# A two-layer decoder trunk: three sub-layer boundaries taken one token tile at a time, the feed-forward in blocks of 512, attention in pairs of heads

## The chip, the cores and the metric

The kernel runs on one core of a Trainium2 chip. TensorE (PE) multiplies, VectorE (DVE) and ScalarE (ACT) do the elementwise work and empty PSUM, GpSimd (POOL) does little, and SyncE (SP) issues nearly all weight loads. PSUM has eight banks, ps0 to ps7, of 128 x 512 floats. The metric is the device time in microseconds (us), the median of several runs; the time before is 1700.63 us.

## The reference, cut to what matters

The input is one sequence of 256 tokens of 1024 floats, so there are two tiles (t = 0, 1) of 128 tokens. All is float32.

```python
# layer 0
u = modulate(rms_norm(x, g_mix[0]), shift, scale)        # shift, scale, gate from c @ w_ada + b_ada
y = concat([dilated_attention(q, k, v), s5_mixer(s_in)]) @ w_out     # 8 heads of 64
x = x + gate * y
u = modulate(rms_norm(x, g_ffn[0]), shift, scale)
x = x + gate * ((silu(u @ w_gate) * (u @ w_up)) @ w_down)            # 1024 -> 2816 -> 1024
# layer 1
u = modulate(rms_norm(x, g_mix[1]), shift, scale)
x = x + gate * (sparse_attention(u @ w_in) @ w_out)      # indexer picks 64 keys, 16 heads of 64
u = modulate(rms_norm(x, g_ffn[1]), shift, scale)
x = x + gate * mixture_of_experts(u)                     # router picks 2 of 8 experts
out = rms_norm(x, g_final)
```

## The kernel before, in words

It is written engine by engine: each engine has its own program in a fixed order, and semaphores tie them together. The order of the work on an engine is the order of its code.

- **Weights.** SP loads items of up to 2 MB into a ring of five slots. A slot is loaded again once its last user has signalled. For the plain float32 projections the signal is `weights_used`, sent by the first PE instruction after the last use (`release`).
- **Split products.** The dense feed-forward, the input projection of layer 1 and the experts multiply in a rounded 32-bit format with three products (`mm3`, L783 to L785). Each weight chunk (a quarter of an item) is split by ACT into `w_hi` (`high`, L1492) and by DVE into `w_lo` (`low`, L1803). There are four chunk buffers, so chunk q can be split only when PE has finished chunk q-4 (`chunk_done`). The other products are plain float32.
- **Modulation vectors.** `c @ w_ada` comes in 24 pieces. `matvec` (L808, L814) multiplies one piece with four groups of 32 columns of the PE array, `part_out` on ACT copies the sums out, and `columns_of` (L822) or `gate_of` (L828) on PE spreads them. The pieces are sown between other work: one beside each head of layer 0, one beside every second head of layer 1, four around the end of the dense feed-forward.
- **A head of attention.** `scores` (PE, L867, contraction over 64 rows), `mask_max` (DVE), `exps` (ACT, L1505), `weights_sum` (DVE), `probs` (ACT, L1514), `probsT` (PE transposes, L789), `probsT_out` (ACT, L1526), `weigh` (PE, L891 to L893, into 64 of the 128 output partitions). Even heads use the lower 64 rows or partitions, odd heads the upper 64. The softmax buffer `sm` has three places, scores go to ps0 and ps1 in turn, and two heads fill one bank that `head_out` copies.
- **A sub-layer boundary.** The last projection ends in four groups of matmuls, one for each token tile and half of the columns. `residual` (DVE, L1885, L1887) multiplies by the gate into an SBUF buffer and adds to `h`. `norm_stats` (ACT) waits for all four, squares and sums both tiles (L1457) and takes both roots (L1460). `norm_scale` (DVE, L1814) scales both tiles, `norm` (PE) transposes 16 blocks of 128, `norm_split` (DVE, L1828) applies the modulation in eight instructions of 256 columns, `norm_hi` (ACT, L1485) and DVE (L1832) split the result into `x_hi` and `x_lo`, and then the split products begin. In front of the router `norm_out` shares the modulation between ACT and DVE, and nothing is split.
- **The dense feed-forward.** 2816 columns in eight blocks of 352. For each block: gate product, up product, silu and product, transposes, down product (three row groups of 128, 128 and 96).
- **The end.** After the experts both tiles are added up, both are normalised, and one store of 1 MB writes the output.

## Time and profile before

| what | us |
|---|---|
| median of three runs | 1700.63 (1700.23 to 1701.93) |
| the profiled execution | 1697.09 |
| its span | 1695.3 |
| PE busy | 1583.3 (93%) |
| DVE busy | 1265.8 (75%) |
| ACT busy | 1045.0 (62%) |

The chain that ended last runs over PE for 81% of the span. About 1000 us of it, from 668 us on, are the experts, where the PE row shows 24.3 to 25 us busy in each 25 us. The first 668 us hold layer 0, the dense feed-forward and the attention of layer 1, with gaps at the boundaries. "PEclk" is the clock granted to TensorE, as a share of its full speed. A plain float32 matmul appears as two records in the trace.

### The profile page before, as it was taken

What the parts mean: (1) busy time and instruction counts of PE and PEld (TensorE: products, weight loads), DVE (VectorE), ACT (ScalarE), POOL (GpSimd) and SP (SyncE); (2) the same over time, 40 slices, a digit from 0 to 9 for tenths busy, and PEclk for the clock granted to TensorE, in tenths of its full rate; (3) what the DMA queues carried; (4) which work ended last, traced back from release to release, by engine and by line L of the source; (5) the groups of instructions that cost most, each with busy time, mean ns of one, the idle gap of its engine ahead of it and who ended that gap; (6) DMA issues with size and microseconds to landing.
All of it is one profiled execution on the core that took longest, in us unless ns stands there. A gap on an engine that the chain in (4) does not pass through costs nothing.

```text
span 1695.3 us, 22996 instructions
## 1 busy us (share of the span) xinstructions
PE 1583.3 (93%) x7839; PEld 1248.8 (74%) x7840; DVE 1265.8 (75%) x1764; ACT 1045.0 (62%) x1401; POOL 62.5 (4%) x90
## 2 busy tenths in 40 slices
PE   4999979999897986999999999999999999999996
PEld 2645479998784535888888888888888888888884
DVE  6895154554545215989989989989989989989986
ACT  3105154443333624778778778778778778778774
POOL 5341000000000000000000000000000000000000
PEclk9999989999888996999999999999999999999998
DMA  9626555554662745999999989999999999989960
GB/s 322 218 98 246 212 194 171 190 185 167 201 224 100 257 147 196 330 338 367 356 332 366 357 328 365 352 331 372 345 335 374 344 335 368 360 325 363 356 229 26
DMA packets 208055, 469.66 MB, mean 277 GB/s; under 512 B 5316, under 2 KB 26102, under 8 KB 207878
## 3 DMA queue, kind: packets, MB, share of 16 engines
q1 hardware_dynamic: 206960, 466.80, 76.2%
q0 software_dynamic: 400, 1.09, 0.3%
q10 hardware_dynamic: 646, 1.16, 0.2%
q8 instruction: 27, 0.44, 0.1%
q14 instruction: 22, 0.18, 0.0%
HBM read 467.98 MB, written 1.05 MB: 277 GB/s over the span
## 4 chain that ended last, share of the span: by engine, by line
PE 81%; DVE 5%; ACT 4%; issue 2%; DVEq 0%; ACTq 0%
PE ps L783 22%; PE ps L785 21%; PE ps L784 21%; PE ps L789 3%; PE ps L1287 2%; PE ps L808 2%; DVE w_lo L1803 2%; PE ps L853 2%; PE ps L1058 2%; ACT work L1699 1%; PE ps L867 1%; PE ps L822 1%; ACT w_hi L1492 1%; PE ps L1356 1%; PE ps L1357 1%
## 5 line engine op out<-in xcount | busy, mean ns | idle before, releaser
L1803 DVE TENSOR_TENSOR w_lo<-ring,w_hi 128x1024 fp32r<-128x1024 f32 (+4 forms) x600 | 672.8, 1155 | 92.0 <-ACT w_hi L1492 79.4
L1492 ACT ACTIVATE w_hi<-ring 128x1024 fp32r<-128x1024 f32 (+4 forms) x600 | 601.3, 1008 | 216.7 <-PE ps L785 214.4
L783 PE MATMUL ps<-w_hi,e_hi 128*128 128x512 f32 x896 | 356.3, 398 | 9.7 <-DVE w_lo L1803 9.7
L785 PE MATMUL ps<-w_hi,e_lo 128*128 128x512 f32 x896 | 350.4, 391 | 0.0
L784 PE MATMUL ps<-w_lo,e_hi 128*128 128x512 f32 x896 | 349.6, 390 | 0.0
L1803 DVE TENSOR_TENSOR w_lo<-ring_more,w_hi 128x1024 fp32r<-128x1024 f32 x192 | 229.0, 1222 | 40.5 <-ACT w_hi L1492 38.1
L1492 ACT ACTIVATE w_hi<-ring_more 128x1024 fp32r<-128x1024 f32 x192 | 201.6, 1067 | 70.8 <-PE ps L785 70.8
L783 PEld LDWEIGHTS ps<-w_hi,e_hi 128*128 128x128 f32 x896 | 168.7, 188 | 46.3 <-DVE w_lo L1803 13.2
L785 PEld LDWEIGHTS ps<-w_hi,e_lo 128*128 128x128 f32 x896 | 168.6, 188 | 36.6
L784 PEld LDWEIGHTS ps<-w_lo,e_hi 128*128 128x128 f32 x896 | 168.8, 188 | 33.5
L783 PE MATMUL ps<-w_hi,eT_hi 128*128 128x512 f32 x448 | 176.7, 394 | 5.6 <-DVE w_lo L1803 5.6
L785 PE MATMUL ps<-w_hi,eT_lo 128*128 128x512 f32 x448 | 174.7, 390 | 0.0
L784 PE MATMUL ps<-w_lo,eT_hi 128*128 128x512 f32 x448 | 174.5, 390 | 0.0
L783 PE MATMUL ps<-w_hi,x_hi 128*128 128x352 f32 (+5 forms) x352 | 116.7, 332 | 9.5 <-DVE x_lo L1832 4.6
L785 PE MATMUL ps<-w_hi,x_lo 128*128 128x352 f32 (+5 forms) x352 | 115.4, 328 | 0.0
L784 PE MATMUL ps<-w_lo,x_hi 128*128 128x352 f32 (+5 forms) x352 | 115.3, 328 | 0.0
L783 PEld LDWEIGHTS ps<-w_hi,eT_hi 128*128 128x128 f32 x448 | 84.1, 188 | 28.3 <-DVE w_lo L1803 11.8
L785 PEld LDWEIGHTS ps<-w_hi,eT_lo 128*128 128x128 f32 x448 | 84.1, 188 | 18.1
L784 PEld LDWEIGHTS ps<-w_lo,eT_hi 128*128 128x128 f32 x448 | 84.2, 188 | 16.6
L783 PEld LDWEIGHTS ps<-w_hi,x_hi 128*128 128x128 f32 x352 | 69.0, 196 | 11.5 <-DVE x_lo L1832 4.9
L784 PEld LDWEIGHTS ps<-w_lo,x_hi 128*128 128x128 f32 x352 | 69.0, 196 | 0.9
L785 PEld LDWEIGHTS ps<-w_hi,x_lo 128*128 128x128 f32 x352 | 68.8, 196 | 0.7
(286 smaller groups left out, 1674.1 us busy)
## 6 DMA issues: line engine op xcount, KB each, us to landing
ring<-in_moe_w_gate SPq DMA_DIRECT2D x48, 2048.0 KB, 10.0
ring<-in_moe_w_up SPq DMA_DIRECT2D x40, 2048.0 KB, 10.2
ring<-in_moe_w_down SPq DMA_DIRECT2D x32, 2048.0 KB, 10.0
ring<-in_w_ada SPq DMA_DIRECT2D x24, 2048.0 KB, 8.4
ring_more<-in_moe_w_down SPq DMA_DIRECT2D x24, 2048.0 KB, 7.9
ring_more<-in_moe_w_up SPq DMA_DIRECT2D x16, 2048.0 KB, 10.0
ring_more<-in_moe_w_gate SPq DMA_DIRECT2D x8, 2048.0 KB, 9.3
ring<-in_ff_w_gate SPq DMA_DIRECT2D x8, 1408.0 KB, 6.5
```

The costliest lines, as they stand in the source:

```text
L783: mm(o, xh, wh, start=start, stop=False)
L784: mm(o, xh, wl, start=False, stop=False)
L785: return mm(o, xl, wh, start=False, stop=stop)
L789: return nc.tensor.transpose(o, i, ident[0:n, 0:n])
L808: w = mm(ps[bank][j:j + 32, :], c_col[:, k:k + 1].broadcast_to([P, 32]), ap[:, k, :], start=k < 4, stop=False, tile_position=(0, j))
L822: w = mm(ps[bank][:, c + q:c + q + 1], part[:, q * P:(q + 1) * P], sel_col, start=True, stop=True)
L853: w = mm(ps[banks[t]][:, 0:n], xT[:, k, t * P:(t + 1) * P], ap[:, k, 0:n], start=k == 0, stop=k == KD - 1)
L867: w = mm(ps[n % 2][:, KOFF[t]:KOFF[t] + KEYS[t]], qT_[r, hh // 2, t * P:(t + 1) * P], kT_[r, hh // 2, 0:KEYS[t]], start=True, stop=True)
L1058: w = mm(ps[2 * n + t][:, :], catT[:, k, t * P:(t + 1) * P], ap[:, k, :], start=k == 4, stop=k == 3)
L1287: w = mm(o, hn[:, t, d], sel[:, t, :], start=t == 0, stop=t == NT - 1)
L1492: fn(w, src, ACT.Copy).then_inc(hi_ready, 1)
L1803: V.tensor_tensor(w_lo[0:n, c, 0:f], src, w_hi[0:n, c, 0:f].bitcast(F32), ALU.subtract).then_inc(lo_ready, 1)
```

## The change

1. **Heads in pairs.** `scores_pair` issues the scores of an even and an odd head in turn, into ps0 and ps1; `weigh_pair` does the same for the weighted sums. DVE and ACT do `weights_sum`, `mask_max`, `exps`, `probs` of two heads one after the other.
2. **Boundaries by tile.** Residual, squares, root, scaling, transposes, modulation and split are done for tile 0 and then for tile 1. The output projections finish both halves of tile 0 first, and the transposes of tile 0 stand before the last group. The gate product of the first feed-forward block, the first projection of layer 1 (`rows_of`) and the router run by tile. ACT squares and takes roots tile by tile, with a root of a constant ahead (`roots`). The gate product of the residual stays in PSUM.
3. **The feed-forward** is cut into five blocks of 512 columns and one of 256.
4. **Four modulation pieces** change places: two go to the start of the feed-forward, the other two to its end.
5. **The end** is done by tile, with two stores of 512 KB.

```diff
-FB = 8
-FW = FF // FB
-FT = [(0, P), (P, P), (2 * P, FW - 2 * P)]
+FW = 512
+FB = (FF + FW - 1) // FW
+FL = FF - (FB - 1) * FW
...
+            def scores_pair(n, qT_, kT_, pair, first=False):
+                if not first:
+                    pe.wait_ge(max_ready, n)
                 for t in range(NT):
...
+                    for i in range(2):
+                        r = slice(HD * i, HD * i + HD)
+                        w = mm(ps[i][:, KOFF[t]:KOFF[t] + KEYS[t]], qT_[r, pair, t * P:(t + 1) * P],
+                               kT_[r, pair, 0:KEYS[t]], start=True, stop=True)
...
+            def weigh_pair(n, v, pair, cat0):
+                pe.wait_ge(pT_ready, n + 2)
...
+                for cols, keys, tile_, first, last_ in (...):
+                    for i in range(2):
+                        hd = slice((2 * pair + i) * HD, (2 * pair + i + 1) * HD)
+                        w = mm(o[HD * i:HD * i + HD, cols], v[:, tile_, hd], pT[:, (n + i) % 2, keys], start=first, stop=last_)
+                w.then_inc(o_done, 2)
...
-            e_out_part(0, (0, 1, 2, 3))
-            pending[0] = True
-            e_out_part(1, (0, 1, 2, 3))
-            pending[0] = True
-            norm(1)
+            pe.wait_ge(gate_ready, 4)
+            e_out_part(0, 0, (0, 1, 2, 3))
+            e_out_part(1, 0, (0, 1, 2, 3))
+            e_out_part(0, 1, (0, 1, 2, 3))
+            norm(1, 0, 4)
+            e_out_part(1, 1, (0, 1, 2, 3))
+            pending[0] = 2
+            matvec(12, 2)
...
-            rows(ff_first["gate"][2], (0, 1), FW, range(NCI), 0)
+            rows_of(ff_first["gate"][2], 0, FW, 0, 1)
+            norm(1, 1, 4)
+            rows_of(ff_first["gate"][2], 1, FW, 1, 1)
+            matvec(13, 6)
+            pe.wait_ge(part_ready, 13)
             rows(ff_first["up"][2], (2, 3), FW, range(NCI))
+            pe.wait_ge(part_ready, 14)
...
             pe.wait_ge(silu_done, FB * NT)
-            matvec(12, 0)
-            matvec(13, 1)
-            ff_T((FB - 1) * NT)
-            ff_down(ff_last["down"][2], (FB - 1) * NT, False, True)
-            pe.wait_ge(part_ready, 14)
             matvec(14, 0)
             matvec(15, 1)
-            pe.wait_ge(h_ready, 8)
+            ff_T((FB - 1) * NT, FL)
+            ff_down_last(ff_last["down"][2], (FB - 1) * NT)
+            pe.wait_ge(part_ready, 16)
...
+            o_out_part(0, 0)
+            o_out_part(1, 0)
+            o_out_part(0, 1)
+            norm(3, 0)
+            o_out_part(1, 1)
+            pending[0] = 2
+            norm(3, 1)
+            pe.wait_ge(late_in, 16 * 2)
+            router(0)
+            router(1).then_inc(router_done, 1)
...
+            def roots():
+                fn(stat[:, 30:31], eps[:, 0:1], ACT.Sqrt)
...
             item_high(ff_first["gate"][2], *ff_first["gate"][:2], ff_chunk_of(FW))
-            norm_hi(1)
+            roots()
+            for t in range(NT):
+                act.wait_ge(h_ready, 2 * t + 2)
+                rms(h[:, t, :], hn[:, t, :], D, t)
+                if t:
+                    part_out(12, parts1[:, 0, :], 2)
+                norm_hi(1, t)
+            part_out(13, parts1[:, 1, :], 6)
             item_high(ff_first["up"][2], *ff_first["up"][:2], ff_chunk_of(FW))
...
-            residual(4, 0, 0, None, 0)
-            norm_scale(1, 2)
-            dve.wait_ge(mod_ready, 2)
             item_low(ff_first["gate"][2], ff_first["gate"][0], ff_chunk_of(FW))
-            norm_split(1)
+            for t in range(NT):
+                residual(t, 4, 0, (t, 2 + t), 0)
+                dve.wait_ge(h_ready, 2 * t + 2)
+                norm_scale(1, t, 3 + t)
+                dve.wait_ge(mod_ready, 2)
+                norm_split(1, t)
...
-            sp.dma_start(out_tok, final_y).then_inc(out_stored, 16)
+            for t in range(NT):
+                sp.wait_ge(y_final, t + 1)
+                sp.dma_start(out_tok[:, t, :], final_y[:, t, :]).then_inc(out_stored, 16)
```

The first place is the middle of the head loop of layer 1 on PE, two heads before the change. (ada is the buffer of the turned queries, keys and values, uT holds the softmax, work the modulation sums.)

```order
L867 MATMUL ps0<-ada_50 128x128
L867 MATMUL ps0<-ada_50 128x256
L891 MATMUL ps5<-uT_49,ada_50 64x128
L892 MATMUL ps5<-uT_49,ada_50 64x128
L893 MATMUL ps5<-uT_49,ada_50 64x128
L789 MATMUL ps2<-cst,uT_49 128x128 x3
L867 MATMUL ps1<-ada_50 128x128
L867 MATMUL ps1<-ada_50 128x256
L891 MATMUL ps4<-uT_49,ada_50 64x128
L892 MATMUL ps4<-uT_49,ada_50 64x128
L893 MATMUL ps4<-uT_49,ada_50 64x128
L822 MATMUL ps7<-cst,work_52 128x1 x4
```

And the same place after the change, one pair of heads:

```order
L808 MATMUL ps6<-ring,c_col 32x512 x8
L814 MATMUL ps6<-bias_rows,cst 32x128 x4
L858 MATMUL ps0<-ada_50 128x128
L858 MATMUL ps1<-ada_50 128x128
L858 MATMUL ps0<-ada_50 128x256
L858 MATMUL ps1<-ada_50 128x256
L884 MATMUL ps4<-uT_49,ada_50 64x128 x6
L789 MATMUL ps2<-cst,uT_49 128x128 x3
L822 MATMUL ps7<-cst,work_52 128x1 x4
L789 MATMUL ps3<-cst,uT_49 128x128 x3
```

The scores of both heads (L858) now stand side by side, in ps0 and ps1 by turns, and so do the six products with the values (L884).

The second place is PE from the end of the output projection of layer 0 to the first feed-forward products, before the change:

```order
L1058 MATMUL ps0<-ring,ada_50 128x512 x4
L1058 MATMUL ps1<-ring,ada_50 128x512 x4
L1058 MATMUL ps2<-ring,ada_50 128x512 x4
L1058 MATMUL ps3<-ring,ada_50 128x512 x4
L789 MATMUL ps0<-cst,work_52 128x128 x2
```

After it (L1056 is the same projection; L808 and L814 are the modulation piece 12):

```order
L1056 MATMUL ps0<-ring,ada_50 128x512 x4
L1056 MATMUL ps2<-ring,ada_50 128x512 x4
L1056 MATMUL ps1<-ring,ada_50 128x512 x4
L789 MATMUL ps4<-cst,work_52 128x128 x4
L789 MATMUL ps5<-cst,work_52 128x128 x4
L1056 MATMUL ps3<-ring,ada_50 128x512 x4
L808 MATMUL ps2<-ring,c_col 32x512 x8
L814 MATMUL ps2<-bias_rows,cst 32x128 x4
```

Tile 0 (ps0 and ps2) is finished first, its transposes go in before the last group (ps3), and a modulation piece follows.

The third place is ACT at the same boundary, after the change (L1504 is the root of a constant, L1499 squares, L1501 takes roots, L1532 modulates, L1541 splits the activations, L1490 copies modulation sums):

```order
L1504 ACT_TABLE_LOAD
L1504 ACTIVATE stat<-eps 128x1
L1499 ACTIVATE work_52,stat<-h 128x1024
L1501 ACTIVATE stat<-stat,eps 128x1
L1532 ACTIVATE uT_49<-ps4,mod_b,mod_a 128x128 x4
L1541 ACTIVATE x_hi_56<-uT_49 128x4x128 x2
L1499 ACTIVATE work_52,stat<-h 128x1024
L1501 ACTIVATE stat<-stat,eps 128x1
L1490 ACTIVATE ada_50<-ps2 128x512
L1532 ACTIVATE uT_49<-ps6,mod_b,mod_a 128x128 x4
L1541 ACTIVATE x_hi_56<-uT_49 128x4x128 x2
L1490 ACTIVATE ada_50<-ps6 128x512
```

The function table is loaded before the squares and not between squares and root, and the copy of piece 13 (L1490 from ps6) is the last of these rows; the split of the first up item comes behind it (L1548, four instructions).

## Rows read from the trace of the kernel before

**Rows 1.** Windows: start:end, length, busy PE PEld DVE ACT POOL, clock, DMA, GB/s.
```profile
211.79:226.24 14.45, 3.59 (x17) 3.28 (x17) 10.52 (x20) 9.81 (x18) 0.00 (x0) 0.72 0.53 190
226.24:413.38 187.14, 187.14 (x1062) 176.60 (x1062) 93.87 (x136) 82.61 (x133) 0.00 (x0) 0.99 0.56 186
421.34:431.37 10.03, 10.03 (x36) 7.80 (x36) 2.19 (x3) 0.58 (x2) 0.00 (x0) 0.83 0.70 227
431.37:449.86 18.49, 12.09 (x98) 8.96 (x97) 13.79 (x28) 10.37 (x20) 0.00 (x0) 0.82 0.87 294
541.95:604.08 62.13, 59.17 (x408) 34.16 (x408) 13.93 (x93) 40.95 (x132) 0.00 (x0) 0.91 0.67 233
631.86:648.62 16.76, 9.01 (x48) 8.68 (x48) 4.86 (x9) 6.98 (x11) 0.62 (x1) 0.68 0.44 157
1675.50:1690.10 14.60, 3.63 (x9) 2.48 (x8) 8.21 (x12) 5.03 (x8) 0.00 (x0) 0.73 0.01 3
```

**Rows 2.** Timeline of PE, heads of layer 0: start, us, instruction, idle before.
```profile
133.31 0.93 PE L867 MATMUL ps<-ada 64*128 64x128 f32 x8 [0.83 <-ACT ada L1551]
...
150.34 1.92 PE L808 MATMUL ps<-ring,c_col 128*32 128x512 f32 x16
...
152.42 0.92 PE L867 MATMUL ps<-ada 64*128 64x128 f32 x4
153.27 0.43 PE L891 MATMUL ps<-uT,ada 128*64 128x128 f32 x2
...
154.07 1.05 PE L822 MATMUL ps<-cst,work 128*128 128x1 f32 x8
154.98 0.53 PE L789 MATMUL ps<-cst,uT 128*128 128x128 f32 x3
155.44 1.92 PE L808 MATMUL ps<-ring,c_col 128*32 128x512 f32 x16
```

**Rows 3.** Timeline of PE, the modulation pieces of layer 1's second and last pair.
```profile
551.06 2.63 PE L808 MATMUL ps<-ring,c_col 128*32 128x512 f32 x16
...
595.62 1.92 PE L808 MATMUL ps<-ring,c_col 128*32 128x512 f32 x16
```

**Rows 4.** Timeline of ACT, one head of layer 1, from probsT_out to probs.
```profile
570.97 0.50 ACT L1526 ACTIVATE uT<-ps 128x384 f32<-128x384 f32 x1
...
572.22 0.80 ACT L1514 ACTIVATE uT<-uT,stat 128x128 f32<-128x128 f32 x2
```

**Rows 5.** Timeline of all engines at the boundary to the feed-forward.
```profile
213.24 1.06 ACT L1457 ACTIVATE work<-h 128x1024 f32<-128x1024 f32 x1 [21.45 <-DVE h L1887]
...
215.44 1.28 ACT L1460 ACT_TABLE_LOAD   x1
216.74 0.30 ACT L1460 ACTIVATE stat<-stat,eps 128x2 f32<-128x2 f32 x1
...
221.81 3.70 DVE L1828 TENSOR_SCALAR uT<-ps,mod_a,mod_b 128x256 f32<-128x256 f32 x8
...
225.43 2.76 DVE L1832 TENSOR_TENSOR x_lo<-uT,x_hi 128x256 fp32r<-128x256 f32 x8
```

**Rows 6.** Timeline of PE, split products of 512 and of 256 columns.
```profile
421.65 0.39 PE L784 MATMUL ps<-w_lo,mT_hi 128*128 128x512 f32 x1
421.88 0.40 PE L785 MATMUL ps<-w_hi,mT_lo 128*128 128x512 f32 x1
...
453.70 0.28 PE L784 MATMUL ps<-w_lo,x_hi 128*128 128x256 f32 x1
453.82 0.28 PE L785 MATMUL ps<-w_hi,x_lo 128*128 128x256 f32 x1
```

**Rows 7.** DMA issues by line: count, KB each, median us from issue to landing.
```profile
ring<-in_w_ada SPq DMA_DIRECT2D x24, 2048.0 KB, 8.4
...
out<-work SPq DMA_DIRECT2D x1, 1024.0 KB, 4.8
```

**Rows 8.** The page's costliest groups: the split of weights on DVE and ACT.
```profile
L1803 DVE TENSOR_TENSOR w_lo<-ring,w_hi 128x1024 fp32r<-128x1024 f32 (+4 forms) x600 | 672.8, 1155 | 92.0 <-ACT w_hi L1492 79.4
L1492 ACT ACTIVATE w_hi<-ring 128x1024 fp32r<-128x1024 f32 (+4 forms) x600 | 601.3, 1008 | 216.7 <-PE ps L785 214.4
```

More of the change, by code:

```diff
@@ L1487, in high, with norm_hi @@
+            def norm_hi(n, t):
+                norm_out(n, t, 4)
+                act.wait_ge(uT_ready, KD * (2 * n + t))
+                for half in range(2):
+                    ks, ts = slice(4 * half, 4 * half + 4), slice(t * P, (t + 1) * P)
+                    fn(x_hi[:, ks, ts], uT[:, ks, ts], ACT.Copy).then_inc(x_hi_ready, 1)
             def high(q, c, src, n=P):
@@ L1557, in _ @@
             th = lambda c: hn.rearrange("p t d -> p (t d)")[:, c * S:(c + 1) * S]
[L1558 to L1566 removed]
+            exps(1, False)
+            for pair in range(A_HEADS // 2):
+                a = 2 * pair
+                probs(a)
+                probs(a + 1)
+                if pair:
+                    part_out(4 + a - 1, parts_b[:, 1, :], 6, a - 1 if a >= 3 else 0)
+                if pair == 3:
+                    gate_out(0, 0, 7, 6)
+                if pair == 0:
                     for c in range(4):
@@ L2065, in _ @@
+            for t in range(NT):
+                dve.wait_ge(h_ready, 4 + 2 * t + 2)
+                norm_scale(2, t, 5 + t)
+            columns(0, 1, 10, 2)
             dve.wait_ge(mod_ready, 3)
```

615 lines of the change are left out of this document (315 added, 300 removed).

## The prediction, made before the change was run

> **What bounds the kernel now.** I read the windows by stage first. PE is busy in all of the 187.14 us of the feed-forward, and in 59.17 of the 62.13 us from the first head product of layer 1 to its output projection; in the four stretches between sub-layers it is busy 3.6 of 14.45, 12.1 of 18.49, 9.0 of 16.76 and 3.6 of 14.60 us [rows 1]. So a gain comes either from PE's own instructions becoming fewer or shorter, or from the chains over DVE and ACT that stand in those four gaps. The timeline of PE then shows what a head is made of [rows 2, 3], that of ACT how long the softmax chain is [rows 4], and that of all engines what stands in a gap [rows 5]. The experts, some 1000 us, are not touched: PE-bound before and after, so nothing is booked there.
>
> The profiled execution took 1697.1 us, 3.5 less than the median of 1700.6. The sum is made against the first and carried to the second.
>
> **Heads of layer 0.** One head takes 5.10 us of PE (150.34 to 155.44): the modulation piece 2.08, scores 0.85, weighted sum 0.80, columns 0.91, transposes 0.46 [rows 2]. Do two heads' scores really run beside each other? The trace has it once: where heads 0 and 1 stand next to each other, eight records take 0.93 us, and four records of a single head take 0.92 [rows 2]. The upper and the lower 64 rows overlap fully. The modulation piece gives the same for output columns: its 16 records of 512 columns go to four groups of 32 columns and take 1.92 us in all [rows 2], while one plain float32 product of 512 columns, moved as four passes at the 0.2275 us of a split product [rows 6], would be 0.9 us, and eight of them 7. So a pair saves one scores and one weighted sum, 0.85 + 0.80. Three pairs of scores in the loop and four weighted sums: 5.8 us. Against it, in the middle pairs DVE has two reciprocal blocks in one piece and ACT copies modulation sums only after both heads' probabilities, so the second piece of a pair starts late; I take 0.7 us twice. Bounds: no overlap and these waits (+1.4), or full overlap and none (-5.8). Value -4.3, near the row that shows the overlap.
>
> **Heads of layer 1.** Six pairs take 44.56 us (551.06 to 595.62), 7.43 each [rows 3]. PE's content falls by 1.65 to 5.7. But now the chain counts: probsT_out to probs of one head is 2.05 us on ACT [rows 4], and ACT does, from the last transpose of a pair, probsT_out 0.4, exps twice 1.8, head_out 0.3, probs twice 1.4, part_out 0.5, in all 4.4, before PE may do the columns (0.9) and the last transposes (0.5): 5.9 with the handovers. The pair period is 5.9: 6 x 1.5 = 9.2 us. At the start the first weighted sum moves into the next pair and the clock is low (0.91 over the stretch [rows 1]): 2.5 us; at the end 0.4. Value -12.1; bounds -14.0 (5.7 per pair) and -1 (no overlap).
>
> **Feed-forward.** A split product of 512 columns follows its forerunner after 0.23 us (0.2275 over long runs), one of 256 after 0.12 [rows 6]. After: gate and up 480 x 0.2275 + 96 x 0.12 = 120.7, five down products 240 x 0.2275 = 54.6, forty transposes at 0.1, together 179.3. Before: 187.14 at a mean clock of 0.99, which is 1.9 lost to the low clock [rows 1], so 185.2. Value -5.9. DVE is 94 of 187 us busy and the DMA share 0.56 [rows 1], which hides the larger items; bounds -4 and -7.
>
> **Boundary to the feed-forward.** Before: 14.45 idle or transposing [rows 1] plus the 1.9. After, beside the products themselves: tile 0's residual, one square (1.1, half of 213.24 to 215.44 [rows 5]), root 0.3, scaling 0.9 hide behind the third of the last four groups but for 0.5; transposes 1.5; piece 12 2.08; transposes of tile 1 1.5. DVE's residual of tile 1 stands behind the split of tile 0, so tile 1 is ready some 3.0 after PE has finished tile 0's gate product and tile 1's transposes. Then piece 13, 2.08. ACT copies its sums before it splits the first up chunk: 0.6 + 1.0 + 1.2 + handovers, a stall of 3.1 [rows 8]. A pause of 3.1 us in the old kernel, just ahead of 421.34, was followed by a low clock: 36 products that need 8.19 us took 10.03 at 0.83 [rows 1]. I book 1.8 after each of the two pauses. Sum 17.4 against 16.4: +1.0. So this boundary, with the most surgery, gives nothing. Bounds -5 (no low clock, no stall) and +5.
>
> **End of the feed-forward.** Before 17.99 (413.38 to 431.37). After: pieces 14 and 15 cost the same 4.0 as 12 and 13 did; piece 15 goes into the slot of the last up item and is issued after its split, some 6 us before PE wants it, with 8.4 to landing [rows 7]: 1.0 on average of 0 to 2.4; transposes and the shorter splits 3.0; the down product 24 x 0.2275 = 5.5 instead of 8.2; low clock 1.8. Sum 15.3, -2.7. Bounds -5 and 0.
>
> **Boundary to layer 1.** Before: 18.49, then 48 products of 256 columns in 7.5, part of them at the low clock: 26.0. After: the residuals on DVE take as long as before, but tile 0's square and root lie inside them, the table load (1.28 [rows 5]) ahead of them, and the two modulation pieces are gone from this stretch. Tile 0's first products can start at about 13.9, tile 1's end at 21.2. Value -4.8; bounds -7 and -2.
>
> **Router.** Before 16.76 after the projection [rows 1]. After: transposes of tile 0 inside the projection 1.2, then for tile 1 residual 1.5, square and root 1.5, scaling 1.0, transposes 1.2, modulation 0.4, router products 5.5 as now. Sum 12.3, -4.5. The two expert loads that waited for the projection's slots are both issued at the router's first product; the experts begin some 25 us later, against 8 to 10 us per load, so nothing is booked. Bounds -7 and -2.
>
> **The end.** Before 14.60 to the store's issue [rows 1] and 4.8 for 1 MB [rows 7]. After: root of tile 0 while tile 1 is squared, second store issued 2.2 earlier; it carries half: between 2.4 and 4.8 us, taken as 3.6. Value -3.4; bounds -4.6 and -1.
>
> Two rules are weighed here; the sum does without them. The load of the function table takes 1.28 us and the root follows at once, at 216.74 [rows 5]. The Trainium skill, page "ScalarE: Activation LUTs", section "What ACT_TABLE_LOAD costs", books a further 1.38 us drain for every switch: by it three loads moved out of the gaps would be worth 8.0 and not 3.8, 4 us more. The 1 MB store took 4.8 us [rows 7], of which nothing in these rows says how much depends on size. The Trainium skill, page "DMA: Bandwidth & Descriptors", section "Anatomy of one DMA", fits about 2 us that no size changes, for transfers issued by GpSimd; if it held for this store, half of it would take 3.4 us by estimate, 0.2 less than in the sum, while pure proportion would give 2.4.
>
> **Sum.** -4.3 - 12.1 - 5.9 + 1.0 - 2.7 - 4.8 - 4.5 - 3.4 = -36.7: 1697.1 becomes 1660.4, and the median 1700.6 becomes 1664.
>
> **Rivals.**
> 1. *The pairs do not overlap*, since operands in one softmax buffer or one output bank (both halves of ps4) forbid it. For it: all evidence of overlap is from other instructions or from one place. Against: [rows 2]. Layer 0 +1.4, layer 1 -1: the time is 1664 + 5.7 + 11.1 = 1681. 0.10.
> 2. *By tile in name only*: DVE's fixed order makes each tile wait for the other, so the four gaps stay, and pieces 12 and 13 come on top. Heads and feed-forward alone give -22.3, gaps 0 to +4: 1678 to 1682. 0.12.
> 3. *The gaps shrink so far that the clock stays high*: the pauses turn out shorter than those that were followed by a low clock. The three low stretches booked (3 x 1.8) and the router's products at full clock (5.5 to about 2.8): -36.7 - 5.4 - 2.7 = -44.8, 1656. 0.20.
> 4. *Slower*: the pauses at the start of the feed-forward keep the clock low for the whole of it. A product of 512 columns at half clock costs 0.2 us more; from 185 such products on the gain is used up, and if all 720 were slow the time would be 1664 + 144 = 1808. Against: after each gap in the old trace the clock came back (0.99 over the feed-forward [rows 1]). 0.03.
>
> The forecast has 0.55. Its own range is 1657 to 1671; to hold 8 in 10 I go to 1652 below, which takes in most of rival 3, and to 1679 above, which takes in part of rival 2. No change is what a measurement cannot tell from 1700.6 within 0.2%, 3.4 us. Faster 0.95, same 0.02, slower 0.03.
>
> **What would show it.** In the new trace: the scores' eight records in about 0.9 us and pairs of layer 1 every 5.9 us (7.3 refutes the overlap, 5.7 the ACT chain as the bound); gate and up of a 512 block without a pause; two pauses of PE of some 3 us around the first gate product of tile 1, the second ended by the split of the first up chunk; the output projection of layer 1 ending 1.2 later after its start and the router 12 after it; the last store issued 2 us earlier. The prediction is wrong if the experts' stretch changes from its 1007 us, or if the boundary to the feed-forward is several us shorter or longer than the old one.

## The result, and the profile after

The changed kernel takes 1663.03 us (median of four runs, 1659.71 to 1666.01) against 1700.43 in the same session: ratio 0.9783, 95% interval 0.977 to 0.9795. The prediction said 1664, range 1652 to 1679. The profiled execution took 1659.71 us, its span is 1657.9 against 1695.3, so 37.4 us shorter. The stages can be laid side by side; each boundary is the same point of the work in both traces (the two pieces at the end of the feed-forward are 12 and 13 before and 14 and 15 after, and behind the last down product the first instruction after it is taken, whichever that is), and the last column is what the prediction's terms give for the stretch.

| stretch | before | after | difference | forecast |
|---|---|---|---|---|
| start to the first modulation piece of the heads | 145.25 | 147.52 | +2.3 | 0 |
| heads of layer 0 | 36.91 | 31.97 | -4.9 | -4.3 |
| output projection, boundary, feed-forward | 231.22 | 224.19 | -7.0 | -4.9 |
| end of the feed-forward | 17.99 | 13.97 | -4.0 | -2.7 |
| boundary to layer 1 and its projections | 110.58 | 105.77 | -4.8 | -4.8 |
| heads of layer 1 | 62.13 | 50.66 | -11.5 | -12.1 |
| output projection, router, first gather | 64.23 | 61.43 | -2.8 | -4.5 |
| experts | 1007.90 | 1008.01 | +0.1 | 0 |
| end | 19.09 | 14.38 | -4.7 | -3.4 |
| sum | 1695.3 | 1657.9 | -37.4 | -36.7 |

The windows of the changed kernel, with the columns of [rows 1]:

```profile
47.04:60.34 13.30, 13.30 (x49) 11.01 (x49) 8.89 (x4) 2.98 (x6) 0.00 (x0) 0.79 1.05 387
...
222.40:229.64 7.24, 7.24 (x25) 5.54 (x25) 0.45 (x1) 0.00 (x0) 0.00 (x0) 0.76 0.99 388
234.79:246.79 12.00, 11.99 (x53) 9.94 (x54) 6.51 (x7) 7.67 (x9) 0.00 (x0) 1.00 0.51 177
412.09:417.65 5.56, 5.56 (x25) 4.58 (x25) 1.65 (x3) 2.17 (x4) 0.00 (x0) 1.00 0.49 145
...
529.03:574.08 45.05, 40.13 (x393) 22.06 (x392) 12.21 (x76) 35.75 (x119) 0.00 (x0) 0.98 0.90 319
574.08:602.60 28.52, 28.52 (x72) 12.91 (x72) 6.35 (x12) 4.40 (x9) 0.00 (x0) 1.00 0.04 13
602.60:615.30 12.70, 8.62 (x41) 8.50 (x40) 3.67 (x8) 4.24 (x8) 0.62 (x1) 0.62 0.55 183
```

The first row holds the 48 projection products of layer 0, at a mean clock of 0.79. In the kernel before they ran at 1.00 and took 10.63 us. The next three rows follow three pauses of PE: 3.01, 3.01 and 2.01 us long; only the first was followed by a low clock. The router's row (602.60) is at 0.62.

PE's timeline, one pair of layer 1's heads, which answers to [rows 3]:

```profile
541.25 1.92 PE L808 MATMUL ps<-ring,c_col 128*32 128x512 f32 x16
...
543.32 0.93 PE L858 MATMUL ps<-ada 64*128 64x128 f32 x8
544.17 0.88 PE L884 MATMUL ps<-uT,ada 128*64 128x128 f32 x12
544.98 0.55 PE L789 MATMUL ps<-cst,uT 128*128 128x128 f32 x3
545.77 1.05 PE L822 MATMUL ps<-cst,work 128*128 128x1 f32 x8 [0.24 <-ACT work L1490]
546.69 0.52 PE L789 MATMUL ps<-cst,uT 128*128 128x128 f32 x3
```

Scores of two heads take 0.93 us, the weighing of two heads 0.88. The pieces stand at 529.03, 535.13, 541.25, 547.14, 553.04, 558.93 and 565.78: 5.9 to 6.1 us a pair, as forecast, but for the last one, 6.85, in which PE waits 1.19 us for DVE's modulation columns. In the same pair ACT works without a gap from the last transposes of the pair before to the copy of the modulation sums (L1490), on which PE's columns wait:

```profile
541.35 0.49 ACT L1582 ACTIVATE uT<-ps 128x384 f32<-128x384 f32 x1 [1.22 <-PE ps L789]
...
545.14 0.58 ACT L1490 ACTIVATE work<-ps 128x512 f32<-128x512 f32 x1
```

That is 4.4 us, the forecast figure.

PE's timeline at the three boundaries:

```profile
218.35 1.03 PE L789 MATMUL ps<-cst,work 128*128 128x128 f32 x8
222.40 0.47 PE L783 MATMUL ps<-w_hi,x_hi 128*128 128x512 f32 x1 [3.01 <-DVE x_lo L1917]
...
229.64 1.92 PE L808 MATMUL ps<-ring,c_col 128*32 128x512 f32 x16
...
234.79 0.47 PE L783 MATMUL ps<-w_hi,x_hi 128*128 128x512 f32 x1 [3.01 <-DVE w_lo L1882]
...
407.34 1.92 PE L808 MATMUL ps<-ring,c_col 128*32 128x512 f32 x16 [1.52 <-DMA ring<-in_w_ada]
...
412.09 0.47 PE L783 MATMUL ps<-w_hi,mT_hi 128*128 128x512 f32 x1 [2.01 <-DVE w_lo L1882]
...
417.65 3.63 PE L822 MATMUL ps<-cst,ada 128*128 128x1 f32 x32
424.18 3.67 PE L789 MATMUL ps<-cst,work 128*128 128x128 f32 x16 [2.90 <-DVE work L1896]
431.32 0.39 PE L783 MATMUL ps<-w_hi,x_hi 128*128 128x256 f32 x1 [3.46 <-DVE x_lo L1917]
...
606.77 1.97 PE L789 MATMUL ps<-cst,work 128*128 128x128 f32 x8 [4.08 <-DVE work L1896]
608.53 6.83 PE L1296 MATMUL ps<-w_r,uT 128*128 128x8 f32 x32
```

The two pauses around tile 1's gate product are the forecast ones. The router's 32 products follow the transposes at once, so no wait shows there, yet they take 6.83 us: 0.21 each, at half clock.

### The profile page after: what moved, and what is told of

Its sections match the earlier page's. It is cut to its first block, busy times and chain, and to the rows that moved or that the text cites. A ratio compares the mean times of both kernels' runs of the same rounds, so it can differ in the third digit from the quotient of the medians.

```text
span 1657.9 us, 22266 instructions
## 1 busy us (share of the span) xinstructions
PE 1551.6 (94%) x7619; PEld 1202.9 (73%) x7620; DVE 1259.0 (76%) x1719; ACT 1043.8 (63%) x1374; POOL 62.8 (4%) x90
## 3 DMA queue, kind: packets, MB, share of 16 engines
HBM read 467.98 MB, written 1.05 MB: 283 GB/s over the span
## 4 chain that ended last, share of the span: by engine, by line
PE 78%; DVE 6%; ACT 5%; issue 2%; DMA 0%; DVEq 0%; ACTq 0%
PE ps L783 22%; PE ps L785 21%; PE ps L784 21%; PE ps L789 2%; PE ps L1330 2%; DVE w_lo L1882 2%; PE ps L1289 2%; PE ps L1056 1%; ACT work L1778 1%; PE ps L808 1%; ACT w_hi L1548 1%; ACT uT L1561 1%; PE ps L828 1%; PE ps L1204 0%; PE ps L1399 0%
## 5 line engine op out<-in xcount | busy, mean ns | idle before, releaser
L1882 DVE TENSOR_TENSOR w_lo<-ring,w_hi 128x1024 fp32r<-128x1024 f32 (+2 forms) x576 | 667.4, 1192 | 116.3 <-ACT w_hi L1548 102.5
L1548 ACT ACTIVATE w_hi<-ring 128x1024 fp32r<-128x1024 f32 (+2 forms) x576 | 594.9, 1038 | 210.3 <-PE ps L785 206.7
L1548 ACT ACTIVATE w_hi<-ring_more 128x1024 fp32r<-128x1024 f32 x192 | 201.6, 1067 | 70.6 <-PE ps L785 70.6
L785 PEld LDWEIGHTS ps<-w_hi,e_lo 128*128 128x128 f32 x896 | 168.6, 188 | 36.7
L783 PE MATMUL ps<-w_hi,x_hi 128*128 128x512 f32 (+4 forms) x288 | 104.2, 362 | 11.0 <-DVE x_lo L1917 6.5
L784 PE MATMUL ps<-w_lo,x_hi 128*128 128x512 f32 (+4 forms) x288 | 103.5, 359 | 0.0
L785 PE MATMUL ps<-w_hi,x_lo 128*128 128x512 f32 (+4 forms) x288 | 103.3, 359 | 0.0
L783 PEld LDWEIGHTS ps<-w_hi,x_hi 128*128 128x128 f32 x288 | 55.5, 193 | 19.4 <-issue 10.5
L808 PE MATMUL ps<-ring,c_col 128*32 128x512 f32 x384 | 50.3, 644 | 14.6 <-DMA ring<-in_w_ada 12.9
L785 PEld LDWEIGHTS ps<-w_hi,x_lo 128*128 128x128 f32 x288 | 55.7, 193 | 7.1
```

Source lines behind the costliest of these rows:

```text
L783: mm(o, xh, wh, start=start, stop=False)
L784: mm(o, xh, wl, start=False, stop=False)
L785: return mm(o, xl, wh, start=False, stop=stop)
L808: w = mm(ps[bank][j:j + 32, :], c_col[:, k:k + 1].broadcast_to([P, 32]), ap[:, k, :], start=k < 4, stop=False, tile_position=(0, j))
L1548: fn(w, src, ACT.Copy).then_inc(hi_ready, 1)
L1882: V.tensor_tensor(w_lo[0:n, c, 0:f], src, w_hi[0:n, c, 0:f].bitcast(F32), ALU.subtract).then_inc(lo_ready, 1)
```

## The experiments

All ran in sessions with the kernel before, whose median was 1700.0 to 1701.4 us there; the changed kernel was not run again beside them. Times are medians; the figures in brackets are the ratio to the kernel before and its 95% interval. Each profile was compared stretch by stretch with that of the changed kernel. Edits are against the changed kernel, cut and shortened.

**The heads' halves kept apart.** PE, both layers' middle pairs:

```diff
-scores_pair(n + 2, ...)
-weigh_pair(n - 2, ...)
+for i in range(2):
+    scores_one(n + 2, ..., i)
+    weigh_one(n - 2, ..., i)
```

> Against the changed kernel, in the middle pairs of both layers' heads the four score products of the one head, the three weighing products of the one head, and then those of the other head follow each other, so that no two products on different 64-row or 64-column halves stand side by side; nothing else moves. Theory (the pairs gain because two heads' products run beside each other): 0.85 us of scores and 0.80 us of weighing come back per pair. In layer 1 PE waits only 0.24 to 0.49 us per pair of 5.9 us, so six pairs grow from 5.9 to about 7.1 to 7.3 us (+8), layer 0 by two pairs x 1.65 (+3): about 11 us slower than the changed kernel, 1674. Rival (the gain came from the new order on ACT and DVE, the overlap is worth nothing): the pairs stay at 5.9 us, time within 2 us of 1663.

Measured: 1674.20 us, ratio to the kernel before 0.9847 (0.983 to 0.9863). The pieces of layer 1 stand 7.02 us apart. PE's timeline:

```profile
546.44 1.92 PE L808 MATMUL ps<-ring,c_col 128*32 128x512 f32 x16
...
548.51 0.92 PE L870 MATMUL ps<-ada 64*128 64x128 f32 x4
549.36 0.87 PE L886 MATMUL ps<-uT,ada 128*64 128x128 f32 x6
550.16 0.92 PE L870 MATMUL ps<-ada 64*128 64x128 f32 x4
551.01 0.87 PE L886 MATMUL ps<-uT,ada 128*64 128x128 f32 x6
...
553.46 1.92 PE L808 MATMUL ps<-ring,c_col 128*32 128x512 f32 x16
```

Four records of one head take as long as eight of both did, six as long as twelve. The same products of the same pairs, only not side by side, cost 11 us by the medians, as the theory said. By stretch the heads of layer 0 took 3.3 us more and those of layer 1 7.4 more: of the 16.4 us that the two layers' heads gained, the overlap is the larger part, although the first and last pairs of both layers were left as they were. The Trainium skill, page "TensorEngine Tiling (Array Packing)", section "Key Properties", says that different tiles of the array can load weights and multiply in parallel; these two traces agree, for halves by rows and for halves by columns.

**Transposes of tile 1 earlier**, after the second chunk of tile 0's gate product:

```diff
-rows_of(gate, 0, FW, 0, 1)
-norm(1, 1, 4)
+rows_of(gate, 0, FW, 0, 1, between=lambda: norm(1, 1, 4))   # ahead of chunk 2
```

> Against the changed kernel, PE transposes tile 1's normed rows between the second and third chunk of tile 0's first gate product instead of after the fourth. In the profile DVE had them ready at 216.0 us and PE came to them at 218.35, then waited 3.01 us for x_lo. Theory (that pause is the order on PE, and the low clock behind it, ten products at 0.43 instead of 0.23 us, is the pause's doing): pause 3.01 to about 0.5, low clock gone, -2.5 - 1.8 = -4.3 us, about 1659. Rival (the pause goes but the low clock stays, or comes from something else): -2.5. Rival (the wait moves to the two engines behind: their chain of 3.5 us starts no earlier): 0.

Measured: 1660.46 us (0.9763, 0.9747 to 0.9779). PE's timeline:

```profile
215.96 1.09 PE L789 MATMUL ps<-cst,work 128*128 128x128 f32 x8 [0.28 <-DVE work L1897]
...
220.07 0.47 PE L783 MATMUL ps<-w_hi,x_hi 128*128 128x512 f32 x1 [0.27 <-DVE x_lo L1918]
...
230.84 0.47 PE L783 MATMUL ps<-w_hi,x_hi 128*128 128x512 f32 x1 [3.01 <-DVE w_lo L1883]
```

The pause is gone and piece 13 starts 3.8 us earlier after piece 12; the theory had 4.3. But the feed-forward's end follows piece 13 by 175.7 us instead of 174.0: now the second pause had a low clock behind it (0.86 over 12 us). 1.6 of 3.8 us came back. That need not be the edit's doing: runs that left both pauses alone show the same 175.6 to 175.7 us (table below).

**Piece 13 into the first pause:**

```diff
+matvec(13, 3)
 rows_of(gate, 1, FW, 1, 1)
-matvec(13, 6)
```

> Against the changed kernel, the modulation piece 13 (2.08 us of PE) stands ahead of tile 1's first gate product, in the pause of 3.01 us, and ACT copies its sums ahead of the split of the first up chunk, without having to wait for PE. The piece's load was issued at 211.8 us and took 7.9, so it is there at 219.7, just after PE's transposes. Theory (the two pauses of 3.0 are independent waits, one filled by the piece, one removed): the second pause of 3.01 goes whole since the split of the up weights follows tile 1's chunks one by one; the first becomes 0.9 idle: -2.1 - 3.0 = -5.1, and the ten products at the low clock may come back to full clock, -1.8 more: 1656 to 1658. Rival (the piece's load lands too late and the transposed tile waits for it): first stretch unchanged, -3.0 at most.

Measured: 1656.37 us (0.9732, 0.9716 to 0.9748), four runs within 1.5 us. PE's timeline:

```profile
220.11 1.92 PE L808 MATMUL ps<-ring,c_col 128*32 128x512 f32 x16 [0.34 <-DMA ring<-in_w_ada]
...
222.78 0.47 PE L783 MATMUL ps<-w_hi,x_hi 128*128 128x512 f32 x1 [0.53 <-DVE x_lo L1916]
...
402.20 1.92 PE L808 MATMUL ps<-ring,c_col 128*32 128x512 f32 x16 [2.95 <-DMA ring<-in_w_ada]
```

Both pauses are gone and no low clock is left: from piece 12 to the feed-forward's end 186.0 us instead of 193.0. Of these 7.0 the end of the feed-forward gave 3.0 back: piece 15's load was waited for 2.95 instead of 1.52 us, and the last down product took 7.15 instead of 5.56 us (mean clock 0.76). The second of these two also comes without the edit (see "What scatters").

**Products that nobody reads, in three waits** (result to a free bank):

```diff
+for _ in range(count):
+    mm(ps[bank], ident, cst[:, C_CAU:C_CAU + 512], start=True, stop=True)
```

> Against the changed kernel, PE is given products whose result nobody reads (128x128 by 512 columns, float32, about 0.91 us each at full clock) in three places where it waits: three before and three after the transposes at the boundary to layer 1 (waits of 2.90 and 3.46 us), seven in the wait of 9.09 us ahead of layer 1's first pair of scores, and four in the wait of 4.08 us ahead of the router's transposes. Theory (what follows these waits runs at half clock because PE stood idle): heads of layer 1 start with eight score records in 0.93 instead of 1.65 us and reach the second modulation piece 2 to 3 us earlier; the router's 32 products end 3 to 4 us earlier (6.83 us now); the first products at the boundary to layer 1 take 0.12 instead of 0.21 us each, 1 to 1.5 us: in all -6 to -8 us, 1655 to 1657. Rival (the low clock at these places costs nothing, the chains over DVE and ACT set the end): within 1 us of 1663. Rival (the products themselves run at half clock and overrun the waits): slower, up to +4.

Measured: 1658.14 us (0.9742, 0.9726 to 0.9759). Place by place: ahead of the router it worked, the experts begin 30.2 us after the output projection's end instead of 32.8. Ahead of the heads of layer 1 the eight score records took 0.93 instead of 1.65 us, but the second piece started no earlier, since PE then waited for ACT, and that piece ran at half clock in 3.64 us. There it cost 1 us. At the boundary to layer 1 it brought 1.2 us (from the last down product to the heads' first piece 93.4 us instead of 94.6). At the start, where nothing was changed, the projection products took 10.63 us as in the kernel before, and layer 0's first piece came 2.9 us earlier. But the feed-forward and its end, which were not changed either, took 2.7 and 3.5 us more. So this profiled execution was no faster than that of the changed kernel (1661.11 and 1659.71 us), and the profile doesn't account for the lower median.

**Piece 15 behind the last transposes:**

```diff
 matvec(14, 0)
-matvec(15, 1)
 ff_T(last)
+matvec(15, 1)          # and its part_out behind the split of the down weights
```

> Against the changed kernel, at the end of the feed-forward PE transposes the last block's rows ahead of modulation piece 15 and not behind it, and ACT copies that piece's sums after the split of the last down weights and not before. In the profile of the changed kernel PE waits 1.52 us for the piece's load, and 2.01 us for the split before the last down product at 412.09 us. Theory (the two waits stand one after the other although they could run beside each other): the last down product starts at about 409.5, -2.6 us, and with no pause of 2 us right ahead of it; about 1660. Rival (the split of the down weights is late for another reason, its load or the buffers): 0. Rival (a pause less, but the piece's own pause is now next to the transposes' and the clock falls for the down product): -1.

Measured: 1659.95 us (0.9761, 0.9745 to 0.9777). The end of the feed-forward (piece 14 to the columns behind the last down product) took 11.44 instead of 13.97 us: -2.5, the two waits did run one into the other.

**The first projection's split ahead of the residuals:**

```diff
 roots()
+item_high(o_in[0])                 # ACT
 norm_stats(2)
...
+item_low(o_in[0], chunks 0, 1, 2)  # DVE, ahead of residual(0)
```

> Against the changed kernel, at the boundary to layer 1 the first projection's weights are split ahead of the residuals: on ACT right after the root's function table is loaded, where it stands idle for 6.34 us, and on DVE three of the four chunks ahead of the residual and the fourth behind the norm's columns. Theory (2.5 us of DVE's splits at 426.01 stand in the chain from the last down product to the first projection product, which is 13.7 us long): three of the four leave it, tile 0's split follows 1.9 us sooner, -1.9 us, first projection product 11.8 us after the last down product. Rival (PE's 16 transposes, 3.67 us at the low clock, are what the split waits for): -0.5 or less. Rival (DVE's three chunks delay the residual, since the buffer of the third is free only when the last down product is nearly done): 0 to +1.

Measured: 1660.42 us (0.9762, 0.9746 to 0.9778). PE's timeline:

```profile
417.51 4.22 PE L822 MATMUL ps<-cst,ada 128*128 128x1 f32 x32
424.04 3.48 PE L789 MATMUL ps<-cst,work 128*128 128x128 f32 x16 [2.31 <-DVE work L1896]
429.24 0.35 PE L783 MATMUL ps<-w_hi,x_hi 128*128 128x256 f32 x1 [1.73 <-DVE x_lo L1917]
```

11.73 us from the last down product to the first projection product instead of 13.67: -1.9 as expected.

**Layer 1's columns behind both heads' transposes:**

```diff
 probsT(n)
-ada_step(pair)
 probsT(n + 1)
+ada_step(pair)
```

> Against the changed kernel, in layer 1 PE does the modulation columns behind the probabilities' transposes of both heads of a pair and not between them, and ACT copies the gates behind both transposed probabilities. The pair period is 5.89 to 6.12 us, in which PE waits 0.24 to 0.49 us. Theory (PE's own content, 5.65 us, is the bound, and ACT's chain costs only those waits): period 5.65 to 5.75, six pairs -1 to -1.5 us, 1662. Rival (ACT's chain of 5.9 us as I forecast it is the bound by itself, and the columns' 0.92 us in it): the period goes to what PE has, the same 5.65, so this run tells only whether the waits are the columns' doing; if the period stays at 5.9, the wait is for the exponentials and not for the copied sums.

Measured: 1660.89 us (0.9755, 0.9735 to 0.9775). PE's timeline:

```profile
550.90 1.92 PE L808 MATMUL ps<-ring,c_col 128*32 128x512 f32 x16
...
553.84 0.88 PE L884 MATMUL ps<-uT,ada 128*64 128x128 f32 x12
554.64 0.88 PE L789 MATMUL ps<-cst,uT 128*128 128x128 f32 x6
555.35 0.95 PE L822 MATMUL ps<-cst,work 128*128 128x1 f32 x8
556.23 1.92 PE L808 MATMUL ps<-ring,c_col 128*32 128x512 f32 x16
```

The pair takes 5.33 us with no wait, less than the 5.65 that I had taken for PE's content. So what I expected here was wrong and what the prediction said right: in the changed kernel ACT's chain, with the columns in it, set the 5.9; taken out of it, PE's own 5.33 is the bound. Not all of the 0.56 us between 5.89 and 5.33 is the wait, though. In the changed kernel PE came to the columns 0.79 us after the start of the transposes ahead of them; three transposes take 0.45 where nothing is waited for (546.69 to 547.14), so the wait was worth 0.34; the other 0.2 is that six transposes side by side take 0.71 us (554.64 to 555.35), while three and three took twice 0.45. These shares are estimates from the two traces. The heads of layer 1 are 4.2 us shorter: 2.4 between the second and last piece, 0.6 ahead of them and 1.2 behind. The profiled execution (1660.98 us) shows none of it in its total, since its feed-forward had a low clock behind both pauses (table below) and its last down product had one too.

**Pieces 14 and 15 into buffers that were long free:**

```diff
 for sec, half in HALVES[2:4]:
+    n_item[0] += 2 if half == 0 else 1
     ada_item(1, sec, half)
```

> Against the changed kernel, modulation pieces 14 and 15 are loaded into the two buffers that pieces 12 and 13 left free long before, and not into those of the feed-forward's last gate and up weights; the first two projection items of layer 1 take these. All three loads (1 + 2 + 2 MB) can then be issued at 390 us. Theory (piece 15 is late because its buffer is freed late: issued at 399.42 us, landed at 407.3): at the 390 GB/s of the busy stretches 5 MB take 13 us, the piece is there at 404 and PE, which wants it at 405.8, does not wait: -1.5 us, and where the wait was followed by a low clock for the last down product (7.15 instead of 5.56 us in the run with piece 13 moved) that is safe too; about 1661. Rival (the three loads at once delay the last down weights, wanted by ACT at 410): 0 to +3.

Measured: 1661.07 us (0.977, 0.9754 to 0.9787). The piece in PE's timeline, with no wait before it:

```profile
407.42 1.92 PE L809 MATMUL ps<-ring,c_col 128*32 128x512 f32 x16
```

and the window of the last down product, with the columns of [rows 1]:

```profile
412.16:419.31 7.15, 7.15 (x24) 5.73 (x25) 1.66 (x3) 2.17 (x4) 0.00 (x0) 0.76 1.08 371
```

The wait for the load is gone, and in this execution the last down product had a low clock, 1.6 us, so that the end of the feed-forward took 14.14 us and nothing was gained. That the clock took the gain back is not shown: the same low clock came with the wait still there (see "What scatters").

**One store in place of two:**

```diff
-for t in range(NT):
-    sp.wait_ge(y_final, t + 1)
-    sp.dma_start(out_tok[:, t, :], final_y[:, t, :])
+sp.wait_ge(y_final, NT)
+sp.dma_start(out_tok, final_y)
```

> Against the changed kernel, the output is stored in one transfer of 1 MB once both tiles are scaled, and not in two of 512 KB; root and scaling stay by tile. Theory (the end gained 2.4 us by the earlier second store and 2.3 us by its half size): the stretch from the last expert product's evacuation to the end grows from 14.4 to about 16.6 us, +2.2. Rival (the store's size hardly matters, its fixed time does): +0.5 or less. Rival (one transfer uses its queue better than two): -0.5.

Measured: 1665.96 us (0.9793, 0.9777 to 0.9809). The end took 15.64 instead of 14.38 us. The last rows of this kernel, then those of the changed one, DVE and SP:

```profile
1658.40 1.28 DVE L2433 SCALAR_TENSOR_TENSOR work<-h,stat,gate_row 128x1024 f32<-128x1024 f32 x1
1659.71 0.40 SPq L681 DMA_DIRECT2D out<-work  x1
```

```profile
1653.48 1.74 SPq L682 DMA_DIRECT2D out<-work  x2
1653.56 1.28 DVE L2434 SCALAR_TENSOR_TENSOR work<-h,stat,gate_row 128x1024 f32<-128x1024 f32 x1
```

From DVE's last result to the end of the span (1664.0 and 1657.9): 4.3 us for 1 MB, 3.1 for the half. The end grew by 1.3 us and not by the 2.2 of the theory, and size explains 1.2 of it. The line through the two has 1.8 us at no size (an estimate from these two runs). The Trainium skill, page "DMA: Bandwidth & Descriptors", section "Anatomy of one DMA", books about 2 us that no size changes, for transfers issued by GpSimd. The estimate is near it, but the runs don't settle it. From issue to landing 512 KB took 2.6 us in all the profiles with two stores; 1 MB took 3.9 us here and 4.8 in the kernel before [rows 7]. A line through 2.6 and 3.9 leaves 1.3 us at no size, one through 2.6 and 4.8 only 0.4, close to pure proportion. Why the same 1 MB took 0.9 us less here is open.

**Unread products at the start and ahead of the router:**

```diff
 pe.wait_ge(part_ready, 4)
+idle_work(4, 5)
 s5_transposes()
 ...
 pending[0] = 2
+idle_work(4, 6)
 norm(3, 1)
```

> Against the changed kernel, PE is given four products that nobody reads (0.9 us each) in its wait of 4.01 us for the first norm's columns at 41 us, and four in the wait ahead of the router's transposes, where the run with such products in three places gained 2.6 us. Theory (the first 48 projection products take 12.2 to 13.4 us in the runs in which PE stood idle for 4 to 5 us ahead of them, and 10.63 in the two in which it didn't): 10.63 here, layer 0's first head 2.3 to 2.8 us earlier; with the router -5 us, 1658. Rival (those two runs differ by something else, the time at which the fourth modulation piece landed): -2.6 only. Rival (the idle products raise nothing and delay the transposes): 0 to +2.

Measured: 1660.48 us (0.9772, 0.9757 to 0.9787). PE's timeline at the start and at the router:

```profile
41.19 3.68 PE L820 MATMUL ps<-cst 128*128 128x512 f32 x8
44.71 1.91 PE L789 MATMUL ps<-cst,work 128*128 128x128 f32 x16
47.33 10.63 PE L924 MATMUL ps<-uT,ring 128*128 128x256 f32 x48 [0.71 <-ACT uT L1530]
...
611.47 3.65 PE L1302 MATMUL ps<-w_r,uT 128*128 128x8 f32 x32
```

The projections take 10.63 us and layer 0's first piece comes 2.4 us earlier; the router's products take 3.65 instead of 6.83, and the experts begin 3.7 us earlier after the output projection. Both places did what the theory says, 6 us together. At the end of the feed-forward, where nothing was changed, 4.5 us went: piece 15 waited 2.79 us for its load and ran at half clock, and the last down product had a low clock too (0.76, 7.16 us). The feed-forward before it took 1.6 us more (194.56). So this profiled execution was as long as that of the changed kernel (1659.73 and 1659.71 us); the median is 2.5 us lower. The rival, the time at which the fourth modulation piece landed, doesn't explain this: here it was waited for 2.18 us and in the run with all edits 1.03, against 0.93 in the changed kernel, and one run without these products waited 2.18 us as well and had 12.23 us for its projections; with them it was 10.63 both times.

**Together.**

> Five edits that were run alone stand together: transposes of tile 1 between the chunks of tile 0's gate product, piece 13 ahead of tile 1's gate product, piece 15 behind the last transposes, the early split at the boundary to layer 1, and layer 1's columns behind both heads' transposes. Their stretches are disjoint but for the first two. Theory (what each took out of its own stretch adds up): boundary to the feed-forward -7 to -9, end of the feed-forward -2.5, boundary to layer 1 -1.9, heads of layer 1 -3, in all -14 to -16: profiled 1643, median 1645 to 1648. Rival (a low clock comes back after each pause that is left, as after piece 13 was moved, where 3.0 of 7.0 us were given back): 1650.

Five edits, measured: 1644.21 us (0.968, 0.9665 to 0.9695), 19 below the changed kernel. The theory had 1645 to 1648. Piece 12 to the feed-forward's end 185.6 us (193.0), the end 11.45 (13.97), last down product to first projection product 11.74 (13.67).

> All edits that gained alone: the five of the run with five edits, pieces 14 and 15 in the buffers that were long free, and the idle products at the start and ahead of the router. Theory (additive): five edits -14 to -16, buffers 0 to -1.5 (alone they removed the wait of 1.52 us and the clock took it back), idle products -5: about 1641 to 1645. Rival (low clock comes back elsewhere): 1648.

All edits, measured: 1637.00 us, five runs 1632.89 to 1641.40 (0.9631, 0.9614 to 0.9649), 26 below the changed kernel, where the theory had 1641 to 1645. The feed-forward took 185.6 us again; over its products, and over the last down product, the clock was 1.00:

```profile
211.10:394.65 183.55, 183.10 (x892) 152.28 (x888) 89.42 (x93) 80.42 (x98) 0.00 (x0) 1.00 0.55 197
399.39:404.96 5.57, 5.57 (x28) 4.61 (x25) 3.46 (x6) 4.34 (x8) 0.00 (x0) 1.00 1.07 371
```

**What scatters.** In these profiles the code from piece 12 to the end of the feed-forward is the same but for the edits named. Us from piece 12 to piece 13, and from there to the end:

| kernel | 12 to 13 | 13 to end | sum |
|---|---|---|---|
| changed kernel | 18.94 | 174.04 | 192.98 |
| heads' halves apart | 18.96 | 174.05 | 193.01 |
| transposes early | 15.12 | 175.67 | 190.79 |
| piece 15 late | 17.35 | 174.07 | 191.42 |
| split early | 18.95 | 174.07 | 193.02 |
| buffers | 18.92 | 175.70 | 194.62 |
| unread products (start) | 18.93 | 175.63 | 194.56 |
| unread products (three waits) | 18.96 | 176.75 | 195.71 |
| one store | 20.10 | 176.84 | 196.94 |
| columns last | 20.16 | 176.93 | 197.09 |
| piece 13 early | - | - | 186.02 |
| five edits, all edits | - | - | 185.61, 185.62 |

The same two pauses of 3.01 us cost nothing, 1.6 us, or 2.7 to 2.9 us each in low clock, and no value in between. The windows of tile 1's gate product, behind the first pause, in the run with piece 15 late and in that with the columns last, with the columns of [rows 1]:

```profile
221.90:227.54 5.64, 5.64 (x24) 4.39 (x24) 0.45 (x1) 0.00 (x0) 0.00 (x0) 1.00 1.04 403
222.13:230.58 8.45, 8.45 (x24) 6.45 (x24) 0.46 (x1) 0.00 (x0) 0.00 (x0) 0.64 0.86 337
```

Without the pauses the stretch repeats within 0.4 us.

The last down product scatters in the same way behind its pause of 1.8 to 2.0 us. It took 5.5 to 5.6 us in the changed kernel and in the runs with the halves apart, the split early and one store. It took 7.1 to 7.2 us in six: transposes early, piece 13 early, columns last, buffers, and the two runs with unread products as their only edit. The waits for piece 15 ahead of it were 1.51 to 1.72 us in all of the first group and 1.56 and 1.64 in two of the second.

## Why the prediction was right

**Heads of layer 0, -4.3, and layer 1, -12.1:** measured -4.9 and -11.5. The overlap that stood in one place of the old trace [rows 2] holds everywhere, and the run with the halves apart showed it to be the cause of the larger part, 10.7 us by stretch. The chain on ACT [rows 4] was the bound at 5.9 us; moving the columns out of it showed that PE alone needs 5.33 in that order. Inside the layer 1 term the sizes were off against each other: six periods -7.8 and not -9.2, mostly since the last waits for the columns, and the start -3.5 and not -2.5. The bound of -14.0 for 5.7 us a pair was also added up wrongly: its terms give -13.3.

**Feed-forward -5.9 and boundary +1.0:** together -4.9, measured -7.0. Both pauses are there, each 3.01 us, ended as forecast by x_lo and by the split weights. The low clock was booked behind both; in this execution it came behind the first only. That is 1.8 of the 2.1 us, and the table above says that it is chance: sums for these same instructions went up to 4.1 us higher. No run undoes the blocks of 512, so their share rests on the traces: with both pauses gone the stretch behind piece 12 took 183.55 us, and without piece 13 (2.08), tile 1's transposes (0.93) and PE's waits (0.45) 180.1 are left by estimate, against 179.3 forecast and 185.2 before.

**End of the feed-forward -2.7:** measured -4.0. The load's stall was 1.52, not 1.0; the booked low clock of 1.8 did not come (5.56 us at 1.00). In six other profiles it did, 7.1 to 7.2 us, so 1.8 us of the difference are chance too.

**Boundary to layer 1, -4.8:** the first projection product 13.67 us after the last down product (forecast 13.9), the whole -4.8. DVE's split of the weights was in the chain; the edit that moved it took 1.9 us out.

**Router -4.5:** measured -2.8. The step that failed is "router products 5.5 as now": they took 6.83, all at half clock, behind a pause of 4.08 us; the runs with that pause filled had 4.71, 3.65 and 5.42 us. The output projection with its transposes was 0.8 longer instead of 1.2, and the stretch up to the first expert product 0.4 longer.

**End -3.4:** measured -4.7. The second store took 3.1 us and not 3.6, the old one 5.2 and not 4.8 up to the span's end; its issue came 2.5 us earlier. Of the 2.1 us between 5.2 and 3.1 the run with one store gives 1.2 to the size; the other 0.9 is unexplained.

**What no step had:** +2.3 us at the start. PE was done with columns and transposes at 41 us, stood idle for 4.01 us for DVE's columns, and ran its projections at 0.79. In the kernel before it had waited 2.58 us for the fourth modulation piece, did columns and transposes at half clock until 46.7 us, came to the same columns without a wait, and had its 10.63 us. Of the eleven profiles, this one included, with the changed kernel's code at the start, ten reach the first piece of the heads at 146.7 to 147.7 us and one, which waited 2.69 us for the fourth piece, at 144.6. So the same code gives both; whether the norm by tile makes the longer one likelier was not tried. The two runs with unread products at the start filled exactly this wait, and both had the 10.63 us. That the sum comes so near is luck in part: opposite errors of +2.3, +1.7, -2.1, -1.3 and -1.3 us met.

Of the rivals the first (pairs do not overlap, 1681) is refuted by the run with the halves apart, which gave the overlap up in most pairs and took 1674. The second (gaps stay) is refuted by the boundaries. The third (the clock stays high, 1656) half came true: of its four places two were at full clock. The fourth (the clock stays low for the whole feed-forward) did not come: behind the first pause it was 0.76 over 7.24 us, and behind the second 1.00. By the Trainium skill's table-load rule, weighed in the prediction, the shorter gaps would have been worth 4 us more. The root follows its table load at once in the changed kernel too, and the boundary to layer 1, with a load moved out of it, came out at the -4.8 that was booked without the rule.

What stays open is what decides whether a pause of about 3 us is followed by a low clock. Length alone doesn't: 3.01 had it and had it not at the same place, in code that is the same, and so had 2.0 at the last down product. The work just before the pause doesn't decide it either: it was the same, in the same order, and the waits in it agreed within 0.2 us.

## What to carry to other kernels

Look for instructions that use half of the array by rows or by columns and put those of the other half right beside them; here that was worth 11 us of 1663 without a product less. When work is split by tile, place each tile's transposes so that the chain behind them (here a wait of 3.0 us on ACT and DVE) runs under the other tile's products, and fill what pause is left with independent work, since the pause costs its length and, by chance, nothing or up to 2.9 us more in low clock. Judge such an edit by its own stretch in the trace and not by the median alone: a gain of 2 us or more was hidden in several of these runs by a low clock at another place. And judge a low clock by several profiles of the same code: one profile with it and one without show nothing about the edit between them.

## What the runs showed that was not expected

- PE that is done earlier can lose. The 48 projection products took 12.2 to 13.3 us in ten profiles: behind waits of 4 to 5 us for DVE's columns in eight, of 0.4 and 0.6 us in two. Where PE came to them without such a wait, at half clock up to then, they took 10.63.
- Work whose result nobody reads, 3.6 us of it in a wait of 4.1, gained 2.6 and 3.7 us ahead of the router. Ahead of layer 1's heads the same thing cost 1 us: the score products behind the rest of the wait, 2.88 us, ran at full clock, but the clock fell behind them, and the next modulation piece took 3.64 us where it takes 2.62 in the changed kernel.
- The clock also fell while PE had no wait. In the run with unread products in three waits the router's products started at 1.00 (over 2.1 us) and went on at 0.54, with nothing between them; in the run with all edits it was 0.97 and then 0.50. That is why they took 4.71 and 5.42 us there, and 3.65 where the clock stayed at 1.00.
- Waits for loads that nobody changed moved: piece 15 was waited for 1.05 to 2.95 us. No run shows what sets this.
